# Moving the second slot of the split weight buffers by 64 bytes in a two-layer decoder trunk

## The reference

```python
h = rms_norm(x, mix_pre_g[l]) * (1 + sc_m) + sh_m
z = h @ w_in                      # 7,696 columns, split over the branches and their gates
y = (g_a * y_a + g_b * y_b + g_c * y_c) @ w_o
x = x + g_m * rms_norm(y, mix_post_g[l])
h = rms_norm(x, ffn_pre_g[l]) * (1 + sc_f) + sh_f
y = swiglu(h, ...)                # layer 0: d_ff 2816
y = sum_e combine[:, e] * swiglu_e(h)   # layer 1: 8 experts, d_ff 3584
x = x + g_f * rms_norm(y, ffn_post_g[l])
```

## Time and profile before

| | |
|---|---|
| median of 3 runs | 1874.24 us (1873.97 to 1874.91) |
| profiled execution, its own time | 1875.42 us |
| its span | 1873.7 us |
| PE busy | 1790.7 us, 96% |
| PEld busy | 1586.8 us, 85% |
| DVE busy | 1552.3 us, 83% |
| ACT busy | 1131.6 us, 60% |
| mean granted TensorE clock | 0.982 |

### The profile page before, as it was taken

One profiled execution on the slowest core, in us unless ns is written; L12 is line 12 of the kernel. 1 busy time (PEld: TensorE's weight loads), 2 busy tenths in 40 slices (PEclk: granted clock), 3 DMA queues, 4 the chain that ended last, 5 costly groups with the idle time before them and its releaser, 6 DMA issues.

```text
span 1873.7 us, 28698 instructions
## 1 busy us (share of the span) xinstructions
PE 1790.7 (96%) x10848; PEld 1586.8 (85%) x10849; DVE 1552.3 (83%) x1442; ACT 1131.6 (60%) x951; POOL 190.7 (10%) x156
## 2 busy tenths in 40 slices
PE   2999998899989999988999999999999999999997
PEld 2999998899979999977888888888888888888885
DVE  6998876999557667777888888898898988988986
ACT  3444564433354545655777777777777677777774
POOL 0395001000005900010000000000000000000000
PEclk8999999899999999998999999999999999999999
DMA  9965534699625434443999989989989899898992
GB/s 377 358 239 192 179 136 157 230 382 365 239 93 188 146 132 139 145 148 112 362 370 345 378 337 362 379 323 377 371 330 378 327 369 376 336 373 344 361 373 86
DMA packets 72523, 525.30 MB, mean 280 GB/s; under 512 B 8113, under 2 KB 8241, under 8 KB 8705
## 3 DMA queue, kind: packets, MB, share of 16 engines
q1 hardware_dynamic: 72288, 524.03, 73.8%
q0 software_dynamic: 160, 0.23, 0.0%
HBM read 523.17 MB, written 1.05 MB: 280 GB/s over the span
## 4 chain that ended last, share of the span: by engine, by line
PE 55%; DVE 2%; ACT 0%; issue 0%; DVEq 0%; ACTq 0%
PE bank L1634 33%; PE bank L1649 16%; PE bank L1669 2%; PE bank L1659 1%; PE bank L1371 1%; PE bank L1342 1%; PE bank L1689 0%; PE bank L1690 0%; PE bank L1605 0%; DVE arena L935 0%; DVE arena L912 0%; DVE arena L939 0%; DVE arena L1058 0%; DVE w_lo L869 0%; DVE arena L1050 0%
## 5 line engine op out<-in xcount | busy, mean ns | idle before, releaser
L1119 DVE TENSOR_TENSOR w_lo<-raw,w_hi 128x2048 fp32r<-128x2048 f32 x224 | 510.1, 2291 | 86.4 <-ACT w_hi L744 86.3
L744 ACT ACTIVATE w_hi<-raw 128x2048 fp32r<-128x2048 f32 x224 | 428.6, 1917 | 98.9 <-PE bank L1649 70.4
L1371 PE MATMUL bank<-acts,w_hi 128*128 128x256 f32 x2080 | 375.8, 285 | 35.4 <-DVE acts L925 26.4
L1371 PEld LDWEIGHTS bank<-acts,w_hi 128*128 128x128 f32 x2080 | 323.9, 193 | 40.6 <-issue 29.9
L1634 PE MATMUL bank<-acts 128*128 128x512 f32 x1248 | 304.3, 393 | 0.0
L1634 PE MATMUL bank<-w_hi,acts 128*128 128x512 f32 x960 | 297.2, 391 | 1.5 <-DVE acts L1263 1.5
L1371 PE MATMUL bank<-acts,w_lo 128*128 128x256 f32 x1040 | 293.8, 283 | 0.0
L1119 DVE TENSOR_TENSOR acts<-raw,acts 128x2048 fp32r<-128x2048 f32 x112 | 256.2, 2287 | 20.3 <-ACT acts L744 20.3
L1634 PEld LDWEIGHTS bank<-acts 128*128 128x128 f32 x1248 | 231.3, 188 | 46.7
L744 ACT ACTIVATE acts<-raw 128x2048 fp32r<-128x2048 f32 x112 | 215.1, 1920 | 72.4 <-PE bank L1634 69.9
L1649 PE MATMUL bank<-w_hi,acts 128*128 128x512 f32 x832 | 256.1, 389 | 0.0
(11 more groups left out here) (237 smaller groups left out, 2149.7 us busy)
## 6 DMA issues: line engine op xcount, KB each, us to landing
raw<-in_experts SPq DMA_DIRECT2D x336, 1024.0 KB, 5.0
raw<-in_stream SPq DMA_DIRECT2D x161, 1024.0 KB, 5.8
arena<-in_x_t SPq DMA_DIRECT2D x1, 1024.0 KB, 11.8
out_t<-arena SPq DMA_DIRECT2D x2, 512.0 KB, 2.6
arena<-in_c_row SPq DMA_DIRECT2D x1, 512.0 KB, 4.6
arena<-in_vecs SPq DMA_DIRECT2D x1, 224.0 KB, 2.5
arena<-in_glr_w POOLq DMA_DIRECT2D x2, 64.0 KB, 4.2
arena<-in_a POOLq DMA_DIRECT2D x2, 32.0 KB, 4.4
```

The source lines that it names most:

```text
L744: act.activation(expert_hi[s], raw[:, slot, :], ACT.Copy).then_inc(hi_written, 1)
L1119: dve.tensor_tensor(expert_lo[s], raw[:, slot, :], f32(expert_hi[s]), ALU.subtract).then_inc(raw_taken, 1)
L1371: mm = pe.matmul(out[:, c, :], w[:, 256 * k + P * c:256 * k + P * c + P], (hi if high else lo)[:, k, :], start=(k == 0 and n == 0 and c == 0),
```

## The change

The two slots of `w_hi`, and those of `w_lo`, were two halves of a 3-dimensional tensor. Now each tensor is flat and 16 words (64 bytes) longer, and the second slot starts 64 bytes behind the end of the first. No instruction is added or removed, and no shape changes.

```diff
-        w_hi2 = sb("w_hi", [P, SPLIT, WORDS], F32R)
-        w_lo2 = sb("w_lo", [P, SPLIT, WORDS], F32R)
+        w_hi2 = sb("w_hi", [P, SPLIT * WORDS + SHIFT], F32R)
+        w_lo2 = sb("w_lo", [P, SPLIT * WORDS + SHIFT], F32R)
+        second = slice(WORDS + SHIFT, SPLIT * WORDS + SHIFT)
         ar = sb("arena", [P, A_END])
         acts = sb("acts", [P, 10240 + SHIFT], F32R)
-        w_hi = [w_hi2[:, 0, :], w_hi2[:, 1, :], acts[:, 4096:6144], acts[:, 6144:8192]]
-        w_lo = [w_lo2[:, 0, :], w_lo2[:, 1, :], acts[:, 8192:10240], acts[:, 8192:10240]]
+        w_hi = [w_hi2[:, 0:WORDS], w_hi2[:, second], acts[:, 4096:6144], acts[:, 6144:8192]]
+        w_lo = [w_lo2[:, 0:WORDS], w_lo2[:, second], acts[:, 8192:10240], acts[:, 8192:10240]]
```

## The result

The changed kernel takes 1893.55 us (median of 4 runs, 1892.38 to 1895.11) against 1874.13 (1873.97 to 1874.91, 4 runs): a ratio of 1.0102, 95% interval 1.0086 to 1.0118. It is slower by 19.4 us. The forecast was 1881 in a range up to 1891; the direction was right, the size was not.

The account below looks back on a forecast made before the run. PE, busy 96% of the span, was taken as the bound, through the distance between matmul starts. Mixers' 7.0 us x 0.95 gave 6.6, other terms 0: 1874.2 + 6.6 = 1880.8, forecast 1881 us, range 1867 to 1891.

Parts of the forecast that it names:

- What bounds the kernel: Whole kernel: PE, busy 96% of the span, bounds it; the distance between matmul starts counts, DVE and ACT changes cost 0.
- The places: Weight slots and `acts`: start addresses matter modulo 128 bytes, with `acts` staying at 64 and the experts' views at 0.
- Experts, "I take 0": Experts' slots 0 and 1: 0 us, late loads hide in 227 ns; bounds 2.0 us gain to 17.9 us loss.
- the cover is gone: Experts: late weight loads stop being hidden only if the moving operand is held up.
- the experts lose too: Experts: moving weights 64 bytes off stationary activations stall, 1,344 matmuls by 6.7 ns, 9.0 us more; 1890 us, chance 0.18.
- Fast distances in the mixers: Mixers' slots 0 and 1: 1,556 distances go from 113.3 to 117.8 ns, 7.0 us, of which 95% reach the end.
- Distances at 117.8, "I leave them where they are": Mixers and dense layer, slots 0 and 1: 2,160 distances stay at 117.8 ns, 0 us; bounds 4.8 loss, 9.7 gain.
- The faster rival: Mixers and dense layer: mixed places break the slow rhythm, 2,160 distances return to 113.3 ns, 9.7 us; 1866 us, chance 0.22.
- The skill's rule: PE: moving operand and weights use independent ports, so buffer places are worth nothing and the time stays at 1874 us.

Follow-up runs that it names:

- the second attempt with one part of the change: Kernel before with only slot 1's high part moved by 64 bytes, `w_hi` 256 bytes longer so everything behind keeps its place modulo 256: 1881.23 us, ratio 1.0036.
- the best kernel: Kernel before with borrowed slots 2 and 3 moved in `acts` (high parts 64 bytes, low 192), operands of branches 1 and 2 by 128: 1861.40 us, ratio 0.9926.

## Why the prediction was wrong

**What bounds the kernel.** Right. PE stays without an idle microsecond in the experts, and what the change does there shows in the distance between two matmuls. DVE's low parts are at 2,292 ns and ACT's high parts at 1,919 on the page after, 1 to 2 ns more; no run gave a sign that they matter.

**The places.** This step was wrong. "By the declared sizes the places modulo 128 become ... `acts` keeps 64, the experts' views keep 0": the period is 256 bytes, not 128. Modulo 256 `acts` goes from 192 to 64 and the experts' activations from 0 to 128. I had named this as what would make me wrong, but gave it no price. Moving those activations by 128 costs 17 us in the experts with nothing else changed (986.0 to 1003.3), and by 256 nothing. In the changed kernel the experts' offsets are 128 and 64 for slot 0, 64 and 0 for slot 1; their steps are 230.6 to 230.8 and 233.3 to 235.2. But the right places alone would not have saved the forecast: with the 128 bytes of `acts` taken back, so that only the weight slots move against it, the experts lose 18 us all the same. The step that decides is the next one.

**Experts, "I take 0".** This is the step that failed. The term was 0 and measured 14.9 us, and its reason failed: "A load that is late by 5 ns has 227 ns to hide in". The loads are as long as ever, 188 ns, and it is the matmul that is recorded 5 ns longer, 394 against 389, in the run with both slots moved, where none of the 960 of one line is below 392; the next one starts 6.7 ns later. The prediction named that as the point where the cover is gone, and its bound of 17.9 us held the cost. The rival "the experts lose too" had the mechanism, a moving operand that is held up because of where it starts against the stationary one; its places were those modulo 128, and its 1,344 slow matmuls were too few. After the change 2,313 distances lie between 230 and 244 ns, against 292 before: with the offsets modulo 256 no slot-0 or slot-1 unit stands at 0 throughout, and mixed offsets slow their neighbours too, as the run with `acts` taken back shows.

**Fast distances in the mixers.** Right in the size of the step, though by places that were wrong modulo 256, so in part by luck; wrong in what reached the end. Slots 0 and 1 of the mixers now have 117.8 to 117.9 ns on average where they had 114.5 to 116.3; over the 2,712 steps of slots 0 and 1 in both mixers this is 7.0 us, the figure of the forecast. Durations of 276 ns became few, 149 of 1,408 with `w_hi` where there had been 838, but did not vanish as I had said they would. And the mixers take only 4.5 us longer, not 95% of 7.0: 2.0 in layer 0's and 2.5 in layer 1's. From the dense layer to layer 1's mixer it is 1.5 less, which leaves the 3.0 of the table. As the first row of that table differs by 2 us between traces with the same mixers, the share that reached the end isn't known closely. That the rest went into waits that PE had anyway is my reading, and no run shows it.

**Distances at 117.8, "I leave them where they are".** Right on average, 117.7 to 117.8 in the dense layer.

**The faster rival.** Its mechanism, a triple with mixed places breaking the rhythm, isn't seen in the changed kernel, whose dense layer stays at 117.7 to 117.8 in slots 0 and 1. In the second attempt with one part of the change something like it is: there slot 0 is at 113.4 behind a slot 1 with mixed places. And its size was real: with the high parts of the borrowed slots at 64 as well the rhythm of 117.8 ns is gone from the dense layer, and 13.0 us come back. By the steps some 8.5 us of this are from slots 2 and 3 themselves and some 5 from slots 0 and 1, nearly all in the dense layer.

**The skill's rule.** The time that I drew from it, 1874 whatever the places, didn't come. The Trainium skill ("TensorE: Matmul & The Clock Gate", Step-by-step: what each phase is for) has loads and moving operand on independent ports that take nothing from each other; moving one against the other by 256 or by 128 bytes gives 1874.8 or 1891.9 us. The Trainium skill also says ("SBUF — State Buffer", Who interferes with whom) that PE never waits on anyone. Here the pace of the matmuls depends on both start addresses. Whether PE's two reads of that memory hold each other up, or something else that depends on both addresses does, the runs don't tell.

**Open.** Why 0 is right for 512 moving columns and 64 for 256; `project_tokens` shows that it isn't the exchanged roles alone, but no run changed the number of columns. Why mixed offsets don't add up. What lies between 0 and 64 in the mixers, and between 0 and 32 in the experts. Why 192 costs the experts less than 64. Why units at offset 64 run at 117.8 ns in the mixers of the best kernel; no run looked at it.

## What to carry to other kernels

When PE is the bound, read the distance between two matmuls of one line and shape, and see whether it has levels; if it has, the place of the stationary against the moving operand, modulo 256 bytes, is worth a sweep over a few offsets, for each matmul shape by itself. An edit that makes one buffer longer moves everything declared behind it: write down all the offsets, and for a period larger than the one you believe in, before you call a term zero. And an experiment that moves one thing needs padding that puts the rest back.

## What the runs showed of the hardware that I had not expected

- The time of an fp32r matmul depends on where its two operands start against each other modulo 256 bytes: 128 bytes cost the experts 17 us of 986, 256 bytes nothing (both kernels differ from the one before only in the place of the experts' split activations and of slot 3).
- At a granted clock of 1.00 the worst mean step of 256 columns and that of 512 at offset 64 cost the same 6.7 ns a matmul: 120.0 against 113.3, 233.4 against 226.7. Other offsets cost less on average (2.2 ns at 192 with 512 columns, 4.5 at 192 and 5.4 at 128 with 256), and mixed ones don't add up: high part at 128 and low part at 0 cost slot 0 of the experts 2.1, high at 0 and low at 192 cost it 5.6.
- Offset 0 is slow for 256 moving columns with either operand stationary: 120.0 ns in `project` and 119.7 to 120.0 in `project_tokens`.
- With 512 columns the weight loads keep their 188 ns while the matmuls go from 389 to 394; with 256 columns at offset 0 the loads are at 192.
- With 256 columns the step depends on the unit before too: slot 0 of the dense layer, at offset 64, runs at 117.8 behind a slot 1 at 64 and at 113.4 behind a slot 1 at 128 (high) and 64 (low), though that slot 1 takes 117.8 and 117.9 itself.
